# The low part of each weight packet in one Pool operation or in two

## The reference

```
def swiglu(h, w_gate, w_up, w_down):
    return (jax.nn.silu(h @ w_gate) * (h @ w_up)) @ w_down
...
x = x + 0.5 * swiglu(rmsnorm(x, ffn1_norm[i]), ffn1_w_gate[i], ffn1_w_up[i], ffn1_w_down[i])
...
ug = u_tab[eidx]
act = jax.nn.gelu(jnp.einsum('td,thkd->thk', xb, ug))
vg = v_tab[eidx]
return jnp.einsum('thk,thkd->td', gate * act, vg)
```

## Time and profile before

| | |
|---|---|
| median of 3 runs | 2077.28 us (2076.43 to 2080.91) |
| the profiled execution | 2076.86 us, its span 2075.1 us |
| Pool, low parts | 402 operations of 1024 columns, about 2.4 us each |
| PE busy | 1898.5 us of the span |

### The profile page before, as it was taken

The page is one execution under the profiler, slowest core; times in us unless marked ns, Lnnn a source line. Parts: engine busy times, 40 slices in busy tenths (PEclk is TensorE's granted clock), DMA queues, the critical chain, the costliest instruction groups (busy, mean ns, idle before and its releaser), DMA issues.

```text
span 2075.1 us, 32623 instructions
## 1 busy us (share of the span) xinstructions
PE 1898.5 (91%) x11598; PEld 1491.5 (72%) x11606; DVE 1221.8 (59%) x2345; ACT 948.8 (46%) x1765; POOL 1274.2 (61%) x724
## 2 busy tenths in 40 slices
PE   7999999999999999999999999998997787777777
PEld 6999888999899997799998876796542232222222
DVE  3444554444544475654456874629776677667764
ACT  4444554444544454654447443355544445444443
POOL 6888665888688876188877951267643443433342
PEclk9999999999999999999999999899999999999999
DMA  6665443555466655056564441248999999999997
GB/s 221 183 183 184 141 151 112 176 185 185 145 186 183 186 156 149 21 172 183 183 181 122 126 129 42 82 150 333 421 421 421 421 421 421 421 421 421 421 420 290
DMA packets 98127, 486.13 MB, mean 234 GB/s; under 512 B 11872, under 2 KB 12896, under 8 KB 65008
## 3 DMA queue, kind: packets, MB, share of 16 engines
q1 hardware_dynamic: 60304, 213.30, 33.5%
q0 software_dynamic: 36864, 268.45, 31.2%
q10 hardware_dynamic: 864, 3.15, 0.4%
HBM read 483.81 MB, written 1.05 MB: 234 GB/s over the span
## 4 chain that ended last, share of the span: by engine, by line
PE 68%; DMA 15%; DVE 9%; ACT 5%; issue 3%; POOL 1%; DVEq 0%; ACTq 0%; POOLq 0%
PE ps L168 17%; PE ps L170 16%; PE ps L169 16%; DMA arena<-uv_tab,arena 15%; PE ps L2273 8%; DVE arena L2431 2%; ACT arena L2188 1%; PE ps L304 1%; POOL arena L2323 1%; DVE h L684 1%; PE ps L289 1%; PE ps L296 1%; PE ps L1996 1%; PE ps L1552 1%; PE ps L290 1%
## 5 line engine op out<-in xcount | busy, mean ns | idle before, releaser
L495 POOL TENSOR_TENSOR split<-raw,split 128x1024 fp32r<-128x1024 f32 x364 | 876.9, 2413 | 402.5 <-ACT split L202 393.7
L202 ACT ACTIVATE split<-raw 128x1024 fp32r<-128x1024 f32 x398 | 420.6, 1059 | 610.8 <-PE ps L170 610.8
L168 PE MATMUL ps<-xs,split 128*128 128x256 f32 (+1 forms) x2272 | 648.9, 286 | 3.7 <-DVE arena L1214 1.6
L169 PE MATMUL ps<-xs,split 128*128 128x256 f32 (+1 forms) x2272 | 640.5, 282 | 0.0
L170 PE MATMUL ps<-xs,split 128*128 128x256 f32 (+1 forms) x2272 | 640.2, 282 | 0.0
L2273 PE MATMUL ps<-arena 128*128 128x512 f32 x1024 | 499.7, 620 | 118.3 <-ACT arena L2188 117.5
L2323 POOL DMA_INDIRECT arena<-uv_tab,arena x256 | 275.4, 1076 | 348.7 <-PE ps L2273 320.9
L2273 PEld LDWEIGHTS ps<-arena 128*128 128x128 f32 x1024 | 179.6, 191 | 429.1 <-ACT arena L2188 281.6
L168 PEld LDWEIGHTS ps<-xs,split 128*128 128x128 f32 x2272 | 430.6, 190 | 20.6 <-issue 14.6
L170 PEld LDWEIGHTS ps<-xs,split 128*128 128x128 f32 x2272 | 431.1, 190 | 0.0
L169 PEld LDWEIGHTS ps<-xs,split 128*128 128x128 f32 x2272 | 428.9, 189 | 2.1 <-issue 1.7
(11 more groups left out here) (364 smaller groups left out, 2022.7 us busy)
## 6 DMA issues: line engine op xcount, KB each, us to landing
raw<-wstream SPq DMA_DIRECT2D x402, 512.0 KB, 3.6
arena<-uv_tab,arena POOLq DMA_INDIRECT x256
arena<-small SPq DMA_DIRECT2D x1, 1291.0 KB
arena<-xT SPq DMA_DIRECT2D x1, 1024.0 KB, 5.6
arena<-keys ACTq DMA_DIRECT2D x1, 1024.0 KB, 7.0
arena<-rows ACTq DMA_DIRECT2D x1, 512.0 KB, 4.6
raw<-rows ACTq DMA_DIRECT2D x1, 512.0 KB, 7.9
out<-raw ACTq DMA_DIRECT2D x1, 512.0 KB
```

The source lines that it names most:

```text
L168: pe.matmul(out, w_hi, x_hi, start=start, stop=False, **kw)
L169: pe.matmul(out, w_hi, x_lo, start=False, stop=False, **kw)
L202: act.activation(parts_of(k, m)[0], raw_slot(k, m), ACT.Copy).then_inc(k.hi_done, 1)
L495: pool.tensor_tensor(lo, raw_slot(k, n), hi.bitcast(F32), ALU.subtract).then_inc(k.lo_done, 1)
```

## The change

In all three places where Pool makes a packet's low part, the subtraction over 1024 columns becomes two: columns 0 to 511, and then columns 512 to 1023. Only the second raises `lo_done`. There is no wait between the two.

```
-            pool.tensor_tensor(lo, raw_slot(k, n), hi.bitcast(F32), ALU.subtract).then_inc(k.lo_done, 1)
+            pool.tensor_tensor(lo[:, 0:512], raw_slot(k, n)[:, 0:512], hi[:, 0:512].bitcast(F32), ALU.subtract)
+            pool.tensor_tensor(lo[:, 512:D], raw_slot(k, n)[:, 512:D], hi[:, 512:D].bitcast(F32), ALU.subtract).then_inc(k.lo_done, 1)
```

## The result

| | before | after |
|---|---|---|
| median of the runs | 2078.43 us (2076.43 to 2080.91, 4 runs) | 2067.52 us (2065.38 to 2068.53, 4 runs) |
| the profiled execution | 2076.86 us, its span 2075.1 us | 2067.38 us, its span 2065.4 us |

The ratio is 0.9946, with a 95% interval of 0.9928 to 0.9963. The change makes the kernel 10.9 us faster. I had forecast some 19 us, 2058 us: the direction is right, the time lies 0.5 us above the top of the range, and the gain is little more than half of what I had worked out.

What follows compares the result with a forecast made beforehand. The prediction took PE to bound the kernel (busy 91% of the span). Gains of 20.6 us less losses of 0.2 and 1.0 gave 19.4 us, so 2058 us; own range 2053 to 2062, with rivals 2 and 4 2052 to 2067.

Steps and rivals of the forecast that it cites:

- three heads: Starts of three feed-forward networks: PE's 2.75 us wait for DVE subtraction L684 shortens by 2.2 us each, 6.6 us gained.
- fourth head: Start of the remaining feed-forward network: PE's wait of 0.56 us for L684 goes, 0.6 us gained.
- clock after the heads: PE's drop to 1.2 GHz after each of three 2.75 us waits at network starts disappears: 3 x 1.5, 4.6 us gained.
- tails: Ends of the four feed-forward networks: PE's waits for L684 of 1.05 to 1.12 us vanish entirely, 4.3 us gained.
- gated linear attention: DVE's L989 and L992 are both stalled there and PE waits 1.37 us; 1.2 us gained.
- stick-breaking projection: Five small DVE steps save about 1.1 us each before an eviction, more than PE's 1.58 us wait: 1.6 us gained.
- mLSTM's wait: L1849 and L1860 start under a low part, saving 1.1 us each against PE's 1.66 us wait: 1.7 us gained.
- retrieval: Around 1430 us, eight slower low parts on Pool delay the ninth slot's issue and the final DMA stream: 1.0 us lost.
- rival 2: Waits at network starts shorten, but PE still drops to 1.2 GHz after them: 2063 us, chance 17%.
- rival 4: More than the sum: the slow clock in the mLSTM goes as well, 2054 us, chance 5%.
- Rival 1: Pool's two halves hold DVE off as one, so stalls stay: 2080 us, no change that can be told, chance 17%.
- Rival 3: Pool becomes the bound: at 1.53 us a half, a packet takes 3.06 us against PE's 2.84; 2096 us, chance 4%.

Runs made afterwards that it cites:

- three busy heads: Kernel before, plus ten products of zeros keeping PE busy during its wait at the start of three feed-forward networks: 2078.51 us, ratio 0.9999.

## Why the prediction came out as it did

| term | forecast (us) | measured (us) |
|---|---|---|
| three heads | 6.6 | 3 x (2.75 - 0.59) = 6.5 |
| fourth head | 0.6 | 0.56 before, 0.59 after: 0 |
| clock after the heads | 4.6 | 1.5, 1.4 and 1.5 |
| tails | 4.3 | -0.6 (0.09 + 3 x 0.16 longer) |
| gated linear attention | 1.2 | -0.1 (1.37 to 1.50) |
| stick-breaking projection | 1.6 | 1.6 |
| mLSTM's wait | 1.7 | 0.6 (1.66 to 1.07) |
| retrieval | -1.0 | -0.94 |
| clock elsewhere, to 1331 us | 0 | about -2.6 (below) |

**Pool's half: right.** Its pitch is 1.24 us (352.24 to 353.48), forecast 1.25 to 1.28.

**Heads: right,** in mechanism and size, for the three that waited 2.75 us. The fourth had slipped through before and had nothing to give. The runs with halves only there and everywhere but there put the whole net gain in them.

**The step that failed: the tails.** I wrote "The half under which L684 starts ends 1.12 to 1.2 us sooner than the whole does. The gap is 1.12 us once and 1.05 us three times: all of it, 4.3 us." That let the subtraction start where it had started. But the operation in front of it, which got through with 0.05 us to spare, now missed Pool's start by 0.10 us. What moved it was the packet of Pool before: it ended later, as I had priced for Pool itself (0.1 to 0.15 us) but not for DVE, and L681 therefore took 0.75 us in place of 0.59. PE's waits for the subtraction came to 7.2 us, where I had named 2 or less as the sign of being right. The run with one whole packet ahead of each tail shows it: the waits go, 4.8 us of them. The same at the gated linear attention, whose five operations (1 and 4) are now held by one half after the other:

```profile
268.50 1.29 POOL L495 TENSOR_TENSOR split<-raw,split 128x512 fp32r<-128x512 f32 x1
269.75 1.48 POOL L496 TENSOR_TENSOR split<-raw,split 128x512 fp32r<-128x512 f32 x1
...
268.67 1.40 DVE L990 TENSOR_TENSOR arena<-arena 128x256 f32<-128x256 f32 x1
270.00 4.30 DVE L993 TENSOR_TENSOR arena<-arena 128x64 f32<-128x64 f32 x4
```

In the mLSTM too: two operations of L1867 take 2.95 us together, one behind each half. Tails, linear attention and mLSTM were forecast at 7.2 us and gave -0.1: that is 7.3 of the 9.7 us by which the sum was too high (19.4 against 9.7).

**The clock.** The term for the heads stood: none of the 24 heads that waited 0.59 us, in six profiles, was followed by a fall. So rival 2 (the clock falls after them anyway) is out. What I left out is that it falls elsewhere instead. Windows of the same two stretches, of the kernel after and then of the one before:

```profile
276.00:281.00 5.00, 5.00 (x32) 5.00 (x31) 1.39 (x7) 0.77 (x3) 2.52 (x2) 0.66 0.38 120
804.00:821.00 17.00, 14.30 (x44) 10.42 (x44) 7.71 (x15) 8.69 (x17) 1.10 (x1) 0.60 0.18 56
```

```profile
279.00:284.00 5.00, 5.00 (x43) 4.93 (x43) 1.79 (x9) 2.10 (x4) 2.82 (x2) 1.00 0.36 121
815.00:832.00 17.00, 14.37 (x58) 10.69 (x58) 10.34 (x20) 10.32 (x21) 0.69 (x1) 0.80 0.18 54
```

Behind the linear attention's wait the granted clock is 0.66, where it was 1.00, and PE gets 32 matmuls through in place of 43; in the stick-breaking attention it is 0.60 against 0.80. The table of stretches puts 1.6 and 2.4 us on these two (0.1 of the first is the longer wait), and 1.4 us on the state-space branch; the mLSTM gives about 2.7 us. This last was rival 4 in part, and luck for the forecast, which had put nothing there. 1.7 us of it came in the kernel with halves at the heads only as well, where the mLSTM's packets are whole, so that much is not due to the halves there. Which of these falls comes in an execution isn't settled: the one behind the linear attention came in both profiles of the change, with halves at heads and tails, with three busy heads and with quarters, and in no other kernel. The longer fall in the stick-breaking attention (13.7 us in place of 6.8) came in five of the six profiles with halves in the projection ahead of it, and in none of the seven with whole packets there. So where it came, the 1.6 us that the projection gave were lost again right behind it; that the missing wait brings the longer fall is not shown.

**Rivals.** Rival 1, the halves hold DVE off as one, is refuted on the path: at head, tail and mLSTM one operation got its turn between the halves. The Trainium skill (SBUF — State Buffer, two separate sides) says that the pair of ports is held for a whole instruction; the rows agree, with the subtraction at 1.40 us under a half and 2.42 under a whole. Rival 1 did hold in the retrieval, off the path (below). Rival 3 did not come with halves, 2.5 us a packet against 2.84; with quarters, 2.92 us, its mechanism did.

**The profile and the median.** The profiled executions differ by 9.5 us, the medians by 10.9. The kernel before has a tie at each head that some executions win; 18 of its runs spread from 2065.78 to 2081.86 us. The profiles show one head won at 2076.86 us and none at 2081.48. The lower end is where four won heads would put it, as 2076.86 - 3 x 3.6 = 2066; but no profile caught such a run, so that is only argued. In both profiles of the change all four heads wait 0.59 us, so the luck is out of the heads. My sum took one won head for granted.

## What to carry to other kernels

When an operation of one engine holds off another's, price a shorter one by following the whole chain of held operations, each from its new start, not only the one that the waits name: here the hold moved one operation up and 7 us of forecast gain stayed away. Cut only the operations under which the awaited steps fall (31 of 402 gave 24.6 us, eight 12.4, all 402 gave 10.9 and 11.5, each against the median beside it), and look at the starts on both engines: where they lie within 0.1 us of each other, a change of 0.1 us anywhere ahead decides a wait of 1 to 2 us. Leave the engine that holds others off a pause in each round: at 2.92 us of work in 2.84 DVE mostly still got in, but the three times that it did not, it waited for Pool's next pause, up to 13 us.

## What the hardware did that I had not expected

- In the three traces of the kernel before, a DVE copy that starts before Pool's operation (by 0.02 to 0.12 us) or 2 ns after it gets through in 0.29 us; one that starts 6 to 33 ns after it takes about 2.53 us.
- DVE gets its turn between two operations of Pool at the head, the tail and in the mLSTM, and through 264 quarters in a row, but not always: 13.25 us under quarters in the third network. And in the retrieval of the kernel after, two operations that start under an indirect DMA of Pool pass neither between it and the first half nor between the halves:

```profile
1419.75 1.76 POOL L2326 DMA_INDIRECT arena<-uv_tab,arena  x1
1421.53 1.27 POOL L2310 TENSOR_TENSOR split<-raw,split 128x512 fp32r<-128x512 f32 x1
1422.75 1.26 POOL L2311 TENSOR_TENSOR split<-raw,split 128x512 fp32r<-128x512 f32 x1
...
1412.79 3.20 DVE L2362 TENSOR_TENSOR arena<-arena 128x256 f32<-128x256 f32 x1
...
1420.95 3.12 DVE L2366 CAST arena<-arena 128x32 f32<-128x32 uint32 x1
```

  The copy at 1420.95 ends at 1424.07, 0.06 us after the second half. What decides when DVE is let in was not tried.
- Taking falls of PE's clock away at some places need not shorten the sum: with three heads busy nothing came, with all four 3.1 us by the ratio and 5.6 by the medians, where 4 x 1.5 had been worked out.
